# A fourth buffer for the high halves of the weights in a streaming-encoder kernel, and rows of the normalisations moved into the arena

## What is computed

```python
for l in range(2):
    z = x @ w_in[l]                       # 1024 -> 512 pool + 4 x 512 mLSTM + 8 gates
    y = concat(pool_mixer(z), mlstm(conv_silu(z_q, z_k), z_v, gates) * sigmoid(z_o))
    h = layer_norm(2**0.5 * x + y @ w_out[l], ln1_g[l], ln1_b[l])
    if l == 0: f = (silu(h @ wg) * (h @ wu)) @ wd                # dense, 2816 wide
    else:      f = sum_e combine[e] * swiglu(h, wg[e], wu[e], wd[e])   # top 2 of 8, 3584 wide
    x = layer_norm(2**0.5 * h + f, ln2_g[l], ln2_b[l])
```

## Time and profile before

| | |
|---|---|
| median of three runs | 1446.62 us |
| the profiled execution, its own time | 1443.45 us |
| its span, first to last instruction | 1441.7 us |
| PE busy with matmuls | 1324.5 us (92%) |
| DVE busy | 1124.1 us (78%) |
| ACT busy | 934.4 us (65%) |
| POOL busy | 127.4 us (9%) |
| read from HBM | 422.91 MB, 294 GB/s over the span |
| granted TensorE clock | 0.973 of 2.4 GHz |

### The profile page before, as it was taken

How to read it: one execution, slowest core, us unless ns; L and a number is a source line. 1 busy time by engine, 2 the same in 40 slices (tenths; PEclk the granted TensorE clock), 3 DMA queues, 4 the chain that set the end, 5 groups by cost and what they waited for, 6 DMA issues and landing times.

```text
span 1441.7 us, 17688 instructions
## 1 busy us (share of the span) xinstructions
PE 1324.5 (92%) x6708; PEld 1083.6 (75%) x6708; DVE 1124.1 (78%) x936; ACT 934.4 (65%) x733; POOL 127.4 (9%) x127
## 2 busy tenths in 40 slices
PE   8998999989997899899999999989999999899996
PEld 7898999978886677677766777766777776676773
DVE  6776544467486789897888998687899878799986
ACT  5544444345344777786867777586777878677773
POOL 4433000035520000000000000000000000000001
PEclk9999999999896999999999999999999999999999
DMA  9635555535426899998998999899899989899990
GB/s 331 215 125 180 178 184 197 177 127 177 164 88 222 310 366 348 398 384 316 410 390 303 375 379 399 305 357 364 302 374 377 401 320 409 309 351 385 378 386 31
DMA packets 132905, 425.18 MB, mean 295 GB/s; under 512 B 8992, under 2 KB 11328, under 8 KB 132816
## 3 DMA queue, kind: packets, MB, share of 16 engines
q1 hardware_dynamic: 131168, 419.16, 78.6%
q0 software_dynamic: 1504, 4.76, 1.1%
q10 hardware_dynamic: 144, 0.07, 0.0%
HBM read 422.91 MB, written 1.05 MB: 294 GB/s over the span
## 4 chain that ended last, share of the span: by engine, by line
PE 60%; DVE 21%; issue 9%; ACT 9%; DMA 1%; SPq 0%; ACTq 0%; DVEq 0%
PE bank L1647 16%; PE bank L1649 15%; PE bank L1648 15%; DVE w_lo L1105 15%; ACT w_hi L773 6%; PE bank L1921 2%; PE bank L1947 2%; PE bank L1948 2%; DVE w_lo L1117 2%; DVE arena L1189 1%; PE bank L1943 1%; PE bank L1944 1%; PE bank L1993 1%; DVE arena L1533 1%; PE bank L1980 1%
## 5 line engine op out<-in xcount | busy, mean ns | idle before, releaser
L1105 DVE TENSOR_TENSOR w_lo<-raw,w_hi 128x2048 fp32r<-128x2048 f32 x216 | 487.9, 2287 | 97.6 <-ACT w_hi L773 96.5
L773 ACT CAST w_hi<-raw 128x2048 fp32r<-128x2048 f32 x216 | 408.1, 1910 | 97.1 <-PE bank L1649 71.4
L1647 PE MATMUL bank<-w_hi,parts 128*128 128x512 f32 x824 | 331.2, 402 | 26.1 <-DVE w_lo L1105 18.5
L1947 PE MATMUL bank<-w_hi,parts 128*128 128x512 f32 x672 | 278.8, 415 | 49.0 <-DVE w_lo L1105 41.7
L1648 PE MATMUL bank<-w_lo,parts 128*128 128x512 f32 x824 | 323.4, 392 | 0.0
L1649 PE MATMUL bank<-w_hi,parts 128*128 128x512 f32 x824 | 323.2, 392 | 0.0
L1948 PE MATMUL bank<-w_lo,parts 128*128 128x512 f32 x672 | 264.7, 394 | 0.0
L1117 DVE TENSOR_TENSOR w_lo<-raw,w_hi 128x2048 fp32r<-128x2048 f32 x61 | 143.6, 2357 | 114.4 <-ACT w_hi L788 114.3
L1947 PEld LDWEIGHTS bank<-w_hi,parts 128*128 128x128 f32 x672 | 126.8, 189 | 115.9 <-DVE w_lo L1105 82.7
L1647 PEld LDWEIGHTS bank<-w_hi,parts 128*128 128x128 f32 x824 | 156.0, 189 | 73.4 <-DVE w_lo L1105 21.0
L1105 DVE TENSOR_TENSOR w_lo<-arena,w_hi 128x2048 fp32r<-128x2048 f32 x80 | 182.6, 2286 | 28.0 <-ACT w_hi L773 27.6
(11 more groups left out here) (238 smaller groups left out, 1235.6 us busy)
## 6 DMA issues: line engine op xcount, KB each, us to landing
raw<-in_wu_exp SPq DMA_DIRECT2D x76, 1024.0 KB, 7.4
raw<-in_wg_exp SPq DMA_DIRECT2D x70, 1024.0 KB, 7.2
raw<-in_wd_exp SPq DMA_DIRECT2D x70, 1024.0 KB, 7.3
arena<-in_wd_exp SPq DMA_DIRECT2D x29, 1024.0 KB, 7.6
arena<-in_wg_exp SPq DMA_DIRECT2D x26, 1024.0 KB, 7.5
arena<-in_wu_exp SPq DMA_DIRECT2D x25, 1024.0 KB, 8.2
raw<-in_w_in SPq DMA_DIRECT2D x20, 1024.0 KB, 7.8
tokens<-in_wg_exp SPq DMA_DIRECT2D x16, 1024.0 KB, 7.4
```

The costliest lines, as they stand in the source:

```text
L773: a.copy(w_hi[:, h, :], ring[s]).then_inc(hi_ready, 1)
L1105: v.tensor_tensor(w_lo[:, h, :], ring[s], w_hi[:, h, :].bitcast(F32), ALU.subtract).then_inc(lo_ready, 1)
L1647: mm(psum, left[0], right[0], start=first, stop=False)
L1947: mm(psum, left, right[0], start=first, stop=False)
```

## The change

`w_hi` gets four buffers, `w_lo` keeps three. ACT now rounds unit n when unit n-4 is done and works three units ahead (`HI_AHEAD`); DVE still works two ahead and waits for unit n-3 itself. The buffer `ln_row` is taken out. The rows of norms 1 and 2 go to the place of `v_sb` and `sigT` in the arena, those of norms 3 and 4 to columns 2048 to 4096. So norms 1 and 3 are loaded after the last product of y has been written (`ym_ready`), norm 2 after the tokens of norm 1 as before, and norm 4 after the first scatter product of the tail (`tail_mm`). In layer 1 the first copy into `v_sb` and the first sigmoid into `sigT` wait for the tokens of norm 2. Both buffers together take as many columns as before: 8 KB more per partition for `w_hi`, 8 KB less for `ln_row`.

```diff
+HIGH = 4
 SPLIT = 3
+HI_AHEAD = HIGH - 1
 AHEAD = SPLIT - 1
...
-        w_hi = sb("w_hi", [P, SPLIT, UNIT], F32R)
+        w_hi = sb("w_hi", [P, HIGH, UNIT], F32R)
         w_lo = sb("w_lo", [P, SPLIT, UNIT], F32R)
...
-        ln_row = sb("ln_row", [P, 2, D])
...
+        ln_old, ln_new = (shaped(arena[:, n:n + 2 * D], [2, D]) for n in (at[0] - 2 * D, 2048))
+        ln_rows = {1: ln_old, 2: ln_old, 3: ln_new, 4: ln_new}
...
+        def high(v):
+            return w_hi[:, (MOE_UNIT0 - LATE + v) % HIGH, :]
+
+        def low(v):
+            return w_lo[:, v % SPLIT, :]
...
             pool.wait_ge(landed[AHEAD], 16)
-            load_ln(1)
...
             def token_rows(s, tiles=range(TT)):
 
+                if s % 2:
+                    pool.wait_ge(ym_ready, TT * HEADS * (s + 1) // 2)
+                    load_ln(s)
+                elif s == 4:
+                    pool.wait_ge(tail_mm, 1)
+                    load_ln(s)
                 pool.wait_ge(ln_in, 32 * s)
...
-                if s < 4:
+                if s == 1:
                     pool.wait_ge(tokens_ready, TT * s)
                     load_ln(s + 1)
...
-                round_unit(SLOT[v], v % SPLIT, landing(p, v), done(p, v - SPLIT))
+                round_unit(SLOT[v], high(v), landing(p, v), done(p, v - HIGH))
...
                 act.wait_ge(landed[n % RAW], 16 * (n // RAW + 1))
-                if n >= SPLIT:
-                    act.wait_ge(unit_done, n - SPLIT + 1)
-                a.copy(w_hi[:, n % SPLIT, :], raw[:, n % RAW, :]).then_inc(hi_ready, 1)
+                if n >= HIGH:
+                    act.wait_ge(unit_done, n - HIGH + 1)
+                a.copy(w_hi[:, n % HIGH, :], raw[:, n % RAW, :]).then_inc(hi_ready, 1)
...
+                    if l and c == 0:
+                        act.wait_ge(tokens_ready, TT * 2)
                     a.activation(sigT[:, c, :], bank[c][:, 0:T], ACT.Sigmoid).then_inc(sig_ready, 1)
...
-            for _ in range(AHEAD):
+            for _ in range(HI_AHEAD):
                 ahead()
...
                     if v > LATE or not first:
-                        round_expert(p, v + AHEAD)
+                        if not last or v + HI_AHEAD < PAIR_UNITS + LATE:
+                            round_expert(p, v + HI_AHEAD)
...
-            def subtract_unit(s, h, rounded):
+            def subtract_unit(s, n, rounded, free):
                 dve.wait_ge(hi_ready, rounded)
-                v.tensor_tensor(w_lo[:, h, :], ring[s], w_hi[:, h, :].bitcast(F32), ALU.subtract).then_inc(lo_ready, 1)
+                dve.wait_ge(unit_done, free)
+                v.tensor_tensor(low(n), ring[s], high(n).bitcast(F32), ALU.subtract).then_inc(lo_ready, 1)
...
-                subtract_unit(SLOT[n], n % SPLIT, done(p, n))
+                subtract_unit(SLOT[n], n, done(p, n), done(p, n - SPLIT))
...
                 dve.wait_ge(hi_ready, n + 1)
+                if n >= SPLIT:
+                    dve.wait_ge(unit_done, n - SPLIT + 1)
...
+                    if l and t == 0:
+                        dve.wait_ge(tokens_ready, TT * 2)
                     v.tensor_copy(v_sb[:, t, :], bank[4 + t][:, :]).then_inc(v_ready, 1)
...
-                st.then(v.tensor_tensor(work[:, 1, c], work[:, 1, c], ln_row[:, 0, c], ALU.mult))
-                v.tensor_tensor(tokens[:, 1, c], work[:, 1, c], ln_row[:, 1, c], ALU.add).then_inc(out_ready, 1)
+                st.then(v.tensor_tensor(work[:, 1, c], work[:, 1, c], ln_new[:, 0, c], ALU.mult))
+                v.tensor_tensor(tokens[:, 1, c], work[:, 1, c], ln_new[:, 1, c], ALU.add).then_inc(out_ready, 1)
```

More of the change, by code:

```diff
@@ L164 @@
 SLOT = [s for n in (9, 9, 9, 9, 8, 8, 8, 8, 8, 8) for s in range(n)]
-assert len(SLOT) == PAIR_UNITS and PAIR_UNITS % SPLIT == 0
+assert len(SLOT) == PAIR_UNITS and PAIR_UNITS % SPLIT == 0 and PAIR_UNITS % HIGH == 0
 C_ID, C_TRI, C_ONES = 0, 128, 256
@@ L472, in parts_of @@
         def parts_of(n, width):
-            return tuple(w[:, n % SPLIT, :].rearrange("p (k n) -> p k n", n=width) for w in (w_hi, w_lo))
+            return tuple(w.rearrange("p (k n) -> p k n", n=width) for w in (w_hi[:, n % HIGH, :], w_lo[:, n % SPLIT, :]))
         def chunk_event(l, kind, c):
@@ L535, in landing_extra, with halves @@
             return fetched[s], j * (16 * len(range(s, ITEM_UNITS, RING))) + 16 * (PAIRS * len(uses(s)) + u // RING + 1)
-        def halves(h, width):
-            return tuple(w[:, h, :].rearrange("p (k n) -> p k n", n=width) for w in (w_hi, w_lo))
+        def high(v):
+            return w_hi[:, (MOE_UNIT0 - LATE + v) % HIGH, :]
+        def low(v):
+            return w_lo[:, v % SPLIT, :]
+        def halves(v, width):
+            return tuple(w.rearrange("p (k n) -> p k n", n=width) for w in (high(v), low(v)))
         block = ctx.enter_context(nc.Block())
@@ L737, in token_rows @@
                     pool.wait_ge(xhat_ready, TT * (s - 1) + t + 1)
-                    st.then(g.tensor_tensor(tokens[:, t, :], work[:, t, :], ln_row[:, 0, :], ALU.mult))
-                    g.tensor_tensor(tokens[:, t, :], tokens[:, t, :], ln_row[:, 1, :], ALU.add) \
+                    st.then(g.tensor_tensor(tokens[:, t, :], work[:, t, :], ln_rows[s][:, 0, :], ALU.mult))
+                    g.tensor_tensor(tokens[:, t, :], tokens[:, t, :], ln_rows[s][:, 1, :], ALU.add) \
                         .then_inc(tokens_ready, 1)
-                if s < 4:
+                if s == 1:
                     pool.wait_ge(tokens_ready, TT * s)
@@ L768, in shift_rows, with round_unit @@
                 a.copy(shift[:, 0:NARROW], ident[:, P - NARROW:]).then_inc(shift_ready, 1)
-            def round_unit(s, h, landed_at, free):
+            def round_unit(s, to, landed_at, free):
                 act.wait_ge(*landed_at)
                 act.wait_ge(unit_done, free)
-                a.copy(w_hi[:, h, :], ring[s]).then_inc(hi_ready, 1)
+                a.copy(to, ring[s]).then_inc(hi_ready, 1)
             def round_expert(p, v):
@@ L1050, in round_extra @@
                 def round_extra(u):
-                    round_unit(u % RING, u % SPLIT, landing_extra(j, u), done_extra(j, u - SPLIT if u >= SPLIT else -1))
-                for u in range(AHEAD):
+                    round_unit(u % RING, high(u), landing_extra(j, u), done_extra(j, u - HIGH if u >= HIGH else -1))
+                for u in range(HI_AHEAD):
                     round_extra(u)
                 for u, (_, kind, b, q) in enumerate(EXTRA):
-                    if u + AHEAD < ITEM_UNITS:
-                        round_extra(u + AHEAD)
+                    if u + HI_AHEAD < ITEM_UNITS:
+                        round_extra(u + HI_AHEAD)
                     if q < block_units(b) - 1 or kind == "d":
@@ L1079, in _ @@
             pair(PAIRS - 1, last=True)
-            for v in range(AHEAD, LATE):
+            for v in range(HI_AHEAD, LATE):
                 round_expert(PAIRS, v)
@@ L1116, in subtract_lo @@
                 dve.wait_ge(hi_ready, n + 1)
-                v.tensor_tensor(w_lo[:, n % SPLIT, :], raw[:, n % RAW, :], w_hi[:, n % SPLIT, :].bitcast(F32),
+                if n >= SPLIT:
+                    dve.wait_ge(unit_done, n - SPLIT + 1)
+                v.tensor_tensor(w_lo[:, n % SPLIT, :], raw[:, n % RAW, :], w_hi[:, n % HIGH, :].bitcast(F32),
                                 ALU.subtract).then_inc(lo_ready, 1)
@@ L1948, in one_pass, with unit @@
                 return mm(psum, left, right[1], start=False, stop=last)
-            def unit(h, split, stream, kind, b, q):
+            def unit(v, split, stream, kind, b, q):
                 times = product if stream == "A" else one_pass
@@ L1965, in unit @@
                     width = EXP_WIDTH[b]
-                    w = halves(h, width)
+                    w = halves(v, width)
                     kn = UNIT // width
@@ L2038, in pair @@
                         start_block(stream, kind, b, ROUND - LATE <= u < ROUND)
-                    unit(u % SPLIT, done(p, u), stream, kind, b, q)
+                    unit(u, done(p, u), stream, kind, b, q)
                     if u in at.fold_g:
@@ L2091, in extra @@
                             pe.wait_ge(ysa_ready, i)
-                    unit(u % SPLIT, done_extra(j, u), "A", kind, b, q)
+                    unit(u, done_extra(j, u), "A", kind, b, q)
                 pe.wait_ge(pickc_ready, TT * j + (2 * TT * PAIRS + TT))
@@ L2126, in _ @@
                     pe.wait_ge(elo_b, EXP_BLOCKS * PAIRS)
-                unit(v % SPLIT, done(PAIRS, v), "AB"[k], "d", EXP_BLOCKS - 1, q)
+                unit(v, done(PAIRS, v), "AB"[k], "d", EXP_BLOCKS - 1, q)
             pe.wait_ge(table_ready, 1)
```

6 lines of the change are left out of this document (3 added, 3 removed).

## The result

The changed kernel took 1375.94 us (median of 4 runs, 1373.24 to 1379.32), the kernel before 1446.53 (median of 4, one more than ahead of the change): a ratio of 0.951, 95% interval 0.949 to 0.954, or 70.6 us less. The forecast was 53.4 us less (1393, range 1362 to 1420). The direction and the mechanism held; the gain was a third larger than forecast, and the time lies on the seam between the likeliest case and the rival in which nearly all the waits go.

The account below looks back on a forecast made before the run. No engine was full; the prediction blamed a PE-ACT-DVE relay, with 103.7 us of PE waits for w_lo. Terms -56 + 0 + 1 + 0 + 1.6 = -53.4 took 1443.45 to 1390.0, plus 3.2 gave 1393 us, range 1362 to 1420.

Parts of the forecast that it names:

- the likeliest case: Whole kernel: part of PE's w_lo waits in the expert stage goes, giving 1376 to 1408 us; chance 0.54.
- the rival in which nearly all the waits go: Expert stage: DVE's two-unit lead carries the B half without a gap, gaining 73 to 90 us, 1359 to 1376; chance 0.14.
- The fourth buffer: Expert stage: ACT's 1.9 us between buffer release and subtraction goes, gaining 56 us of 103.7 us of waits.
- The block on which the step was worked out: Expert stage, 24 units from 1049 to 1114 us: 65.0 us, 9.3 of them w_lo waits; 5.0 us saved, 54%.
- the two ends of the worked block: 24 expert units: DVE's busy time allows 6.5 us saved, transfers at 410 GB/s allow 3.6 us.
- DVE's extra wait: Expert stage: 336 added wait instructions on DVE cost 0, with bounds of nothing and 17 us.
- The start: Kernel start: ACT's extra roundings delay q's copies, which DVE reads first; 1 us lost, ends 2.6 gained and 4 lost.
- Norms 1 to 3: Layers before the experts: later-loaded norm rows cost 0, norm 3's covered by 2 to 6 us.
- The tail: Kernel end: norm 4's rows come late and hold POOL and DVE; 1.6 us lost, ends 0 and 6.
- Transfers bind at once: Expert stage: transfers limit a block's saving to 3.6 us or less, stage gain 25 to 40, 1408 to 1424; chance 0.22.
- The floor is already reached: Expert stage: transfers already set its length, so it stays 965 us and the kernel 1447 to 1450; chance 0.03.
- ACT blocked at landings: Expert stage: ACT's earlier rounding waits for landings and delays its silu, 21 us slower, about 1465 us; chance 0.04.

Follow-up runs that it names:

- the rows-alone run: The changed kernel with three w_hi buffers again and ACT two units ahead, norm rows still moved: 1448.29 us, ratio 1.002.
- the experiment on the tail: The changed kernel with ACT rounding two units ahead at the start and norm 4's rows loaded on an earlier PE signal: 1372.65 us, ratio 0.947.
- the half loads: Each expert load moves half its unit: 1371.15 us (ratio 0.949) in the changed kernel, 1442.11 us (0.9995) in the kernel before.
- half the subtraction: The changed kernel with DVE subtracting only 1024 of 2048 columns of each expert unit: 1341.26 us, ratio 0.926.
- its repetition: The changed kernel word for word, timed again on the same chip as a version with three further edits: 1375.12 us, ratio 0.951.
- the run with DVE's order: The changed kernel with DVE subtracting unit u+3 ahead of the hidden product or low halves at two kinds of step: 1369.17 us, ratio 0.946.
- The combination: The changed kernel with the start, tail and DVE-order edits together: 1366.24 us, ratio 0.945.

## Why the prediction was right, and where it was not

**The fourth buffer: the term that was mis-sized.** The step gave 56 us. The stage gained 71.7, and PE's waits for w_lo fell by 70.1, 68% of the 103.7, to 33.6 us and not to the 40 to 60 named. The block on which the step was worked out is not where it missed. The same 24 units now take 59.8 us in place of 65.0, a gain of 5.2 where 5.0 were taken, and their waits for w_lo fell from 9.3 to 3.5:

```profile
1010.80:1070.60 59.80, 58.97 (x262) 46.56 (x261) 58.91 (x39) 50.29 (x31) 0.00 (x0) 1.00 1.02 398
```

What missed is the next step, "On the stage's 103.7 us of waits", which laid this block's share on all of them. By the times at which PE ends the units:

```
                                   gained                 before    after
first 24 units of the four pairs   2.3, 7.1, 8.7, 8.5     295.1     268.5
eight middle blocks of 24          4.5 to 5.0 each        524.6     486.4
last units of the four pairs       0.5, 3.0, 2.1, 1.3     144.8     137.9
```

The eight middle blocks, two of which the worked one lies across, did as forecast. At the changes of pair more was lost before, and more came back: in the first 24 units of the second to fourth pair DVE is busy 58 of 65.8 us after the change, and a unit takes 2.74 us there, which is 382 GB/s: neither of the two ends of the worked block binds. (Taken per unit and not per wait, 5.0 us on 14 blocks of 24 units would have given 70.)

That the block came out at 5.0 is in part luck, since it was the middle between two ends, and one of them isn't there. The transfers take nothing in it: with half the bytes it takes 59.8 us too. DVE's end was the right one, it is busy 58.9 of the 59.8 us, but it had been put 1.3 us too low (58.5). The prediction had itself written down why the transfers need not bind: the units landed in advance. It counted 10 us of that lead and let 2.7 of them go for the earlier rounding. The lead was 13.2 us on the mean and could fall to 7.9, at times to nothing, without a noted wait of ACT for a landing.

**The mechanism, and one part of it taken for granted.** The prediction told buffer and place as one edit: the count waited for "is the same as before", and "what goes is ACT's 1.9 us". Both are so in the changed kernel, and the handover shows it. But the words lay the gain on the buffer's being free. The two runs that part the edit show that the buffer alone gives some 8 of 70 us and the place alone none. The price of the silu ahead of the rounding stood in the earlier trace rows (1073.04, before 1073.96) and was not worked out.

**DVE's extra wait: 0.** Right; the rows-alone run has it and its stage is 1.7 us shorter, not longer.

**The start: 1 us lost.** Right in size, 1.3, but by another reader. ACT rounds the third unit at its landing, ahead of the gates, and the fourth (at 26.18) ahead of the copies of q:

```profile
21.37 1.91 ACT L804 CAST w_hi<-raw 128x2048 fp32r<-128x2048 f32 x1 [3.14 <-DMA raw<-in_w_in]
23.18 0.46 ACT L850 ACTIVATE arena<-bank,gate_b 4x256 f32<-4x256 f32 x1
...
28.50 0.36 PE L1671 MATMUL bank<-x_hi,w_hi 128*128 128x256 f32 x1 [1.19 <-ACT arena L862]
```

The copies start at 27.99, 2.2 us late. The prediction took DVE for the first to need them; it is PE that waits, 1.2 us, for the bank that the copy (L862) frees. The removed 1 MB of rows gives something back: with the rows alone unit 6 ended 1.6 us earlier than before.

**Norms 1 to 3: 0.** The cover at norm 3 held:

```profile
416.56 0.54 POOL L684 DMA_DIRECT2D arena<-in_ln_b  x1
427.59 2.38 POOL L754 TENSOR_TENSOR tokens<-work,arena 128x1024 f32<-128x1024 f32 x1 [10.48 <-DVE work L1349]
```

POOL waits for DVE, not for its rows. What the stages before the experts lost beyond the start, 2.4 us of the 3.7, is no cost of an edit that these profiles can name: the next section has it.

**The tail: 1.6 us lost.** Right in kind, somewhat less in size:

```profile
1358.33 0.69 DVE L1553 TENSOR_TENSOR work<-work,bank 128x512 f32<-128x512 f32 x1 [6.96 <-PE bank L1968]
...
1364.19 2.34 POOL L754 TENSOR_TENSOR tokens<-work,arena 128x1024 f32<-128x1024 f32 x1 [4.48 <-DMA arena<-in_ln_b]
...
1366.52 2.98 DVE L1349 TENSOR_SCALAR work<-work,mv,rstd 128x1024 f32<-128x1024 f32 x1
```

POOL multiplies 5.9 us after the first scatter product is added, 4.9 before and 6.3 by the forecast, released by the rows; DVE's normalisation beside its second operation takes 2.98 us where it took 2.02. From the last unit to the end it is 1.1 us more, but that stretch varies with the scatter products ahead of the rows: 20.2 us in the second profile, and 19.4 to 21.6 in those of the kernels here with four high buffers three ahead. From DVE's normalisation of tile 0 on, which doesn't wait for the rows, it is 11.6 us before and 12.5 and 12.3 in the two profiles of the change: 0.7 to 0.9 us, which the experiment on the tail takes back.

**The rivals.** Transfers bind at once: excluded by the half loads. The floor is already reached: excluded, the stage went from 354 to 382 GB/s, and with half the subtraction to 397. The rule of the Trainium skill, "DMA: Bandwidth & Descriptors", section "Where 436 GB/s comes from", that bounds loads from HBM at about 358 GB/s per core, does not hold in these runs on one core: 397 over 858 us. ACT blocked at landings: no such wait in the changed kernel's profile, and one of 0.3 us in its repetition. Nearly all the waits go: not quite, a third is left; its time was the nearest none the less. DVE stands at 815.5 of 892.8 us, the 91% that was held against it, which was thus no argument against it.

## What to carry to other kernels

Where a spare buffer is added to a relay of engines, move the work that fills it ahead of what waits in that engine's own order, or the buffer stays idle; and price the two apart, as here 8 us against 70. A share of the waits worked out on one stretch holds for stretches like it: here it was right for its block and for eight more, and 15 us too low over the whole, because the changes of pair had other limits. And count what is stored ahead before a transfer rate is taken as a limit: a ring with 13 us of landed units pays for a stage that rises to within 7% of the 410 GB/s that its fullest stretches show (382 of 410).

## What the runs showed of the hardware

**Two engines on a coin's edge.** At norm 2 DVE forms x_lo just when POOL adds its rows. The same program, profiled twice (first the change, then its repetition):

```profile
318.61 2.37 POOL L755 TENSOR_TENSOR tokens<-tokens,arena 128x1024 f32<-128x1024 f32 x1
318.69 4.63 DVE L1166 TENSOR_TENSOR x_lo<-arena,x_hi 128x512 fp32r<-128x512 f32 x4
```

```profile
321.47 2.49 DVE L1166 TENSOR_TENSOR x_lo<-arena,x_hi 128x512 fp32r<-128x512 f32 x4
321.50 9.10 POOL L755 TENSOR_TENSOR tokens<-tokens,arena 128x1024 f32<-128x1024 f32 x1
```

One of the two is stretched, to 4.6 us on DVE or to 9.1 on POOL. Mostly it is the one that starts later, by as little as 0.03 us, but in the run with half loads POOL started first and was stretched. When DVE loses, PE waits, and its granted clock is lower: over 318 to 326 us it was 0.50, 0.58 and 0.58 in the three traces where x_lo was stretched here, and 0.63 to 0.86 in the others (0.85 in the kernel before). Between units 41 and 47, where this lies, the changed kernel lost 2.7 us to the one before, in the repetition 0.5; there x_lo was stretched at norm 1 (4.03 us), and 2.5 us were lost between units 13 and 41. The sum ahead of the experts differs by up to 5.5 us between profiles of kernels that do the same there.

**The clock falls under full load too.** In the run with DVE's order, four stretches in a row:

```profile
1098.00:1104.00 6.00, 6.00 (x36) 5.23 (x35) 4.47 (x3) 3.44 (x4) 0.00 (x0) 1.00 1.02 409
1104.00:1110.00 6.00, 6.00 (x42) 5.46 (x41) 5.03 (x3) 3.56 (x4) 0.00 (x0) 0.99 1.02 408
1110.00:1116.00 6.00, 6.00 (x20) 4.55 (x21) 1.24 (x2) 3.54 (x3) 0.00 (x0) 0.50 1.03 410
1116.00:1122.00 6.00, 6.00 (x27) 4.93 (x26) 5.10 (x3) 4.63 (x4) 0.00 (x0) 0.94 0.86 309
```

PE is shown busy throughout (6.00 of 6 us), 1.00 and 0.99 granted, and then one stretch at 0.50, the lower of its two levels (1.2 GHz): 20 matmuls start in it and not some 40. Such a fall costs about 3 us. The combination, with the same order on DVE, has none there, and that accounts for its shorter stage: 884.4 against 889.5 us, and 3.4 against 8.4 us lost to the clock, so 881 for both without it. What sets such a fall off stays open.
